# A hybrid decoder layer on eight cores: eleven pre-cast experts instead of ten, gathers requested four steps ahead, and the overflow weights fetched in two parts

## The reference, cut to what matters

```python
h = rmsnorm(x, g_mix); proj = h @ w_in                 # D = 1024, 1792 columns
attn = sliding_window_attention(q, k, v, sinks)         # window 128, 8 heads of 64
lru = rg_lru(causal_conv4(lx)) * gelu(lg)               # 512 channels, associative scan
x = x + concat(rmsnorm(attn), rmsnorm(lru)) @ w_out
h2 = rmsnorm(x, g_ffn)                                  # mixture of experts
g_top  = top1(softmax(h2 @ w_rg)); e_top = top2 of the 8 experts of that group
x = x + sum over the two experts: w_tok * (silu(h2 @ Wg[e]) * (h2 @ Wu[e])) @ Wd[e]
gate = sigmoid(rmsnorm(x, g_ple) @ w_ple_gate)          # per-layer embedding
x = x + gate * (p @ w_ple_proj)
return rmsnorm(x, g_final)
```

## Time and profile before

| what | value |
|---|---|
| median of 3 runs | 1447.66 us (1443.44 to 1447.93) |
| the profiled execution: its own time | 1447.09 us |
| its span on the slowest core (core 4) | 1445.4 us |
| spans of the eight cores | 1414.2 to 1445.4 us |
| PE / DVE / ACT / POOL busy over the span | 76% / 48% / 51% / 33% |
| granted clock of TensorE, mean of core 4 | 0.850 |
| DMA queue of GpSimd (software), of SyncE (hardware) | 57.1% and 20.1% of 16 engines over the span |

### The profile page before, as it was taken

How to read it: one execution, slowest core, us unless ns; L and a number is a source line. 1 busy time by engine, 2 the same in 40 slices (tenths; PEclk the granted TensorE clock), 3 DMA queues, 4 the chain that set the end, 5 groups by cost and what they waited for, 6 DMA issues and landing times.

```text
span 1445.4 us, 24745 instructions; the slowest of 8 cores (1414.2 to 1445.4 us)
## 1 busy us (share of the span) xinstructions
PE 1092.8 (76%) x7740; PEld 722.3 (50%) x7834; DVE 698.8 (48%) x1253; ACT 742.1 (51%) x1392; POOL 483.6 (33%) x576
## 2 busy tenths in 40 slices
PE   2535759988979897267697979988988797681892
PEld 1312225555555555156475757766766575550440
DVE  4879995977777864541121212211212121225853
ACT  4778897887877974012232423333333242224882
POOL 3212132332323333024242434433444243220663
PEclk9766777988978978559799989999999899895896
DMA  8999996963705932408999999999989989888422
GB/s 230 193 190 109 107 109 85 189 115 96 132 9 88 144 106 94 184 21 160 204 195 220 175 216 208 204 187 205 234 190 184 223 156 174 174 276 319 163 117 117
DMA packets 69775, 234.93 MB, mean 163 GB/s; under 512 B 23430, under 2 KB 30342, under 8 KB 51472
## 3 DMA queue, kind: packets, MB, share of 16 engines
q0 software_dynamic: 43984, 134.60, 57.1%
q1 hardware_dynamic: 25664, 98.75, 20.1%
HBM read 415.47 MB, written 101.71 MB: 358 GB/s over the span
## 4 chain that ended last, share of the span: by engine, by line
PE 44%; DMA 20%; issue 11%; DVE 9%; ACT 9%; POOL 4%; SPq 1%; another core or an unknown queue 0%; DVEq 0%; ACTq 0%; POOLq 0%
PE ps L1369 13%; DMA sb_R<-h2scr,sb_R 12%; PE ps L1341 7%; PE ps L967 4%; DMA sb_R<-wall,sb_R 3%; DMA sb_R<-w_pg 3%; PE ps L751 3%; PE ps L1324 2%; PE ps L1004 2%; PE ps L1512 2%; PE ps L841 2%; PE ps L903 1%; DMA sb_R<-xin 1%; PE ps L904 1%; PE ps L1245 1%
## 5 line engine op out<-in xcount | busy, mean ns | idle before, releaser
L1369 PE MATMUL ps<-sb_R 128*128 128x256 bf16 x3008 | 343.0, 275 | 5.3 <-DMA sb_R<-wall,sb_R 3.6
L1369 PEld LDWEIGHTS ps<-sb_R 128*128 128x128 bf16 x3008 | 296.0, 99 | 53.3 <-issue 6.7
L1351 POOL DMA_INDIRECT yscr<-sb_R x94 | 94.6, 1006 | 361.1 <-DVE sb_R L1348 344.9
L1374 DVE TENSOR_TENSOR sb_R<-sb_R,ps 128x512 bf16<-128x512 f32 x94 | 64.7, 688 | 296.9 <-PE ps L1369 268.8
L1327 ACT COPY sb_R<-ps 128x1024 bf16<-128x1024 bf16 x94 | 95.1, 1012 | 191.6 <-PE ps L1324 187.3
L1341 PE MATMUL ps<-sb_R 128*128 128x512 bf16 x706 | 171.2, 396 | 4.9 <-issue 2.1
L1348 DVE COPY sb_R<-ps 128x512 f32<-128x512 f32 x94 | 65.0, 692 | 222.5 <-PE ps L1341 140.2
L1373 ACT ACTIVATE sb_R<-ps 128x512 f32<-128x512 f32 x94 | 56.1, 597 | 224.8 <-PE ps L1369 224.7
L1295 POOL DMA_INDIRECT sb_R<-h2scr,sb_R x94 | 97.7, 1039 | 89.3 <-DVE sb_R L1254 60.9
L1341 PEld LDWEIGHTS ps<-sb_R 128*128 128x128 bf16 x752 | 74.5, 102 | 89.0 <-issue 19.8
L1324 PE MATMUL ps<-sb_id,sb_R 128*128 128x128 bf16 x752 | 58.1, 237 | 63.6 <-DMA sb_R<-h2scr,sb_R 63.1
(11 more groups left out here) (234 smaller groups left out, 2085.6 us busy)
## 6 DMA issues: line engine op xcount, KB each, us to landing
sb_R<-wall POOLq DMA_DIRECT2D x66, 1024.0 KB, 23.1
wbf<-wall POOLq DMA_DIRECT2D x30, 1024.0 KB, 46.0
sb_R<-wbf SPq DMA_DIRECT2D x30, 1024.0 KB, 13.2
sb_R<-xin SPq DMA_DIRECT2D x32, 512.0 KB, 20.3
sb_R<-yscr SPq DMA_DIRECT2D x16, 1024.0 KB, 8.1
xscr<-sb_R SPq DMA_DIRECT2D x16, 512.0 KB, 4.1
sb_R<-xscr SPq DMA_DIRECT2D x16, 512.0 KB, 13.4
out<-sb_R SPq DMA_DIRECT2D x16, 512.0 KB, 2.7
```

Source lines behind the costliest of these rows:

```text
L1351: return e.indirect_dma_start(y_d, bass.IndirectOffsetOnAxis(ap=didx[:, blk:blk + 1], axis=0), y.ap, None, bounds_check=breg(e, 2 * T_OWN ...
L1369: ins = e.matmul(pv[:, q * N:(q + 1) * N], lhsT=w_[:, c, f * P:(f + 1) * P], rhs=hT_[:, c, 0:N], start=(c == 0), stop=(c == 7))
L1374: S.op("dve", lambda e: e.tensor_tensor(hid[s % 2][:, fp * 2:fp * 2 + 2, 0:N], sgs[fp][:, 0:2 * N].rearrange("p (q t) -> p q t", q=2), pu. ...
```

## The change

`PC` becomes eleven experts, without 0 and 1, and spread evenly from 2 to 28; the six that are cast behind tiles go behind tiles 0, 2, 4, 6, 8 and 10. Experts 0 and 1 are read as float32 on GpSimd's queue. Gathered rows get a ring of `NG` = 5 and are requested four steps ahead. `wall` is split into `wgu` (gate and up) and `wdn` (down); `load_ov` has two parts with a dependency each: gate and up are requested behind `gateup(s, 1)` of an overflow step, down behind its `down`. Since a fifth gather buffer moves what lies behind it by 1024 words, `wov` now reaches 384 words into the mixer's `Wout`, and the dispatch's temporaries are moved to the place of `hTs`, `hid`, `sgs` and `Y`, over the mixer's `b1024` and `f512` pools. In the tail only 8 of the 16 `ppT` are made ahead (ring of 8), four behind the first group and four behind the second.

```diff
-        PC = [0, 1, 2, 6, 9, 13, 16, 20, 23, 27]
+        PC = [2, 4, 6, 9, 11, 14, 17, 19, 22, 25, 28]
...
-                    S.dma("pool", wbf_d[E, :, sl], wall_d[E, :, sl], writes=[pc_b[E][i]], sembuf=pcs_b[E], after=[mk], kb=1536)
+                    S.dma("pool", wbf_d[E, :, sl], wgu_d[E, :, sl] if i < 2 else wdn_d[E], writes=[pc_b[E][i]], sembuf=pcs_b[E], after=[mk], kb=1536)
...
-                    if gt - 16 in (0, 3, 5, 8, 10):
+                    if gt - 16 in (0, 2, 4, 6, 8, 10):
                         precast(1, mt)
...
         NWG, NWD = 4, 3
+        NG = 5
+        rtb = B("rtmp"); ut_b = B("utri"); qr_b = B("qr"); OHm1_b = B("OHm")
+        OH_b = [B(f"OH{i}") for i in range(4)]; OHr_b = [B(f"OHr{i}") for i in range(4)]
         wg_b = [B(f"wg{i}") for i in range(NWG)]; wu_b = [B(f"wu{i}") for i in range(NWG)]; wd_b = [B(f"wd{i}") for i in range(NWD)]
-        G_b = [[B(f"G{i}{h}") for h in range(2)] for i in range(4)]
+        G_b = [[B(f"G{i}{h}") for h in range(2)] for i in range(NG)]
         hTs_b = [B("hTs0"), B("hTs1")]; hid_b = [B("hid0"), B("hid1")]; sg_b = [B("sg0"), B("sg1")]
-        wov_b = B("wov")
+        wov_b = B("wov"); wovd_b = B("wovd")
         wgs = [R.alloc(8 * 512, BF16, wg_b[i]).rearrange("p (c f) -> p c f", c=8) for i in range(NWG)]
...
         wds = [R.alloc(4 * D, BF16, wd_b[i]).rearrange("p (c d) -> p c d", c=4) for i in range(NWD)]
+        tmp_off = R.off
         hTs = [R.alloc(8 * 256, BF16, hTs_b[i]).rearrange("p (c t) -> p c t", c=8) for i in range(2)]
         hid = [R.alloc(4 * 256, BF16, hid_b[i]).rearrange("p (c t) -> p c t", c=4) for i in range(2)]
         sgs = [R.alloc(512, F32, sg_b[i]) for i in range(2)]
         YP = R.pool(S, "Y", 1024, 5)
         tail_end = R.off
-        Gb = [R.alloc(2 * D, BF16, *G_b[i]).rearrange("p (h d) -> p h d", h=2) for i in range(4)]
+        Gb = [R.alloc(2 * D, BF16, *G_b[i]).rearrange("p (h d) -> p h d", h=2) for i in range(NG)]
         wov = R.alloc(12288, BF16, wov_b)
+        wovd_b.ranges.append((R.off - 2048, R.off)); wov_b.ranges[0] = (R.off - 6144, R.off - 2048)
...
-        R.off = disp_off
-        rtb = B("rtmp"); ut_b = B("utri")
+        R.off = tmp_off
...
-        rtb.ranges.append((disp_off, R.off)); rtb.older = None
+        assert R.off <= tail_end
+        rtb.ranges.append((tmp_off, R.off))
...
-                    return e.indirect_dma_start(Gb[s % 4][:, h, :], None, h2_d,
+                    return e.indirect_dma_start(Gb[s % NG][:, h, :], None, h2_d,
...
-                S.dmaop("pool", fn, reads=[ix_b] + H2d, writes=[G_b[s % 4][h]], kb=256)
...
-        def load_ov(j):
+                S.dmaop("pool", fn, reads=[ix_b] + H2d, writes=[G_b[s % NG][h]], kb=256)
+        def load_ov(j, part):
             if j >= NOVF:
                 return
+            dst, src, wb = ((wov[:, 0:8192], wgur, wov_b), (wov[:, 8192:12288], wdnr, wovd_b))[part]
             def fn(e):
-                return e.indirect_dma_start(wov, None, wallr,
+                return e.indirect_dma_start(dst, None, src,
                                             bass.IndirectOffsetOnAxis(ap=oidx[:, j:j + 1], axis=0),
                                             bounds_check=breg(e, NE * P - 1), oob_is_err=False)
-            S.dmaop("pool", fn, reads=[ox_b], writes=[wov_b], kb=256)
+            S.dmaop("pool", fn, reads=[ox_b], writes=[wb], kb=256)
         def weights_of(st_):
             if st_[0] == "b":
                 E = st_[1]
                 return wgs[E % NWG], wus[E % NWG], wds[E % NWD], wg_b[E % NWG], wu_b[E % NWG], wd_b[E % NWD]
-            return wov_g, wov_u, wov_d, wov_b, wov_b, wov_b
...
-        S.op("pool", lambda e: e.memset(wov.bitcast(F32), 0.0), writes=[wov_b])
-        for i in range(4):
+        S.op("pool", lambda e: e.memset(wov.bitcast(F32), 0.0), writes=[wov_b, wovd_b])
+        for i in range(NG):
             S.op("pool", lambda e, i=i: e.memset(Gb[i].bitcast(F32), 0.0), writes=G_b[i])
...
-        load_ov(0)
-        load(2)
+        load_ov(0, 0)
+        load_ov(0, 1)
+        for s in range(2, NG - 1):
+            load(s)
         trans(0)
         for s in range(nS):
-            if s + 3 < nS:
-                load(s + 3)
+            if s + NG - 1 < nS:
+                load(s + NG - 1)
...
                 down(s - 1)
                 k, j = steps[s - 1]
                 if k == "o":
-                    load_ov(j + 1)
+                    load_ov(j + 1, 1)
                 elif j + NWD < NE and j + NWD >= NPL:
                     load_wd(j + NWD)
             gateup(s, 1)
             k, j = steps[s]
+            if k == "o":
+                load_ov(j + 1, 0)
             if k == "b" and NPL <= j + NWG < NE:
                 load_w(j + NWG)
...
-        THP = R.pool(S, "thp", 128, 16)
+        THP = R.pool(S, "thp", 128, 8)
         TP = R.pool(S, "tp", 256, 1)
         TH = R.pool(S, "th", 128, 2)
         ppTs = []
-        for ot in range(NT):
+        def pp_tile(ot):
...
+        for ot in range(8):
+            pp_tile(ot)
         for g in range(NT // 4):
             xs, h3s = [], []
...
+            if g < 2:
+                for ot in range(8 + 4 * g, 12 + 4 * g):
+                    pp_tile(ot)
```

More of the change, by code:

```diff
@@ L588, in build @@
     brt_d = dt("b_rt", [1, 36], F32, kind="ExternalInput").ap()
-    wall_d = dt("wall", [NE, P, 12288], F32, kind="ExternalInput").ap()
+    wgu_d = dt("wgu", [NE, P, 8192], F32, kind="ExternalInput").ap()
+    wdn_d = dt("wdn", [NE, P, 4096], F32, kind="ExternalInput").ap()
     cst_d = dt("cst", [P, 2 * P + 41], F32, kind="ExternalInput").ap()
@@ L1134, in build @@
         slots = R.alloc(2 * NT); sli = R.alloc(2 * NT, I32); qi = R.alloc(2 * NT, I32); ri = R.alloc(2 * NT, I32)
-        qf = R.alloc(2 * NT); rf = R.alloc(2 * NT); qr_b = B("qr")
+        qf = R.alloc(2 * NT); rf = R.alloc(2 * NT)
         slots3 = slots.rearrange("p (t k) -> p t k", t=NT)
@@ L1138, in build @@
         OHq = [R.alloc(4 * NB).rearrange("p (j n) -> p j n", j=4) for _ in range(2)]
-        OHm1 = R.alloc(4 * NB).rearrange("p (j n) -> p j n", j=4); OHm = [OHm1, OHm1]; OHm1_b = B("OHm"); OHm_b = [OHm1_b, OHm1_b]
-        OH_b = [B(f"OH{i}") for i in range(4)]; OHr_b = [B(f"OHr{i}") for i in range(4)]
+        OHm1 = R.alloc(4 * NB).rearrange("p (j n) -> p j n", j=4); OHm = [OHm1, OHm1]; OHm_b = [OHm1_b, OHm1_b]
         p1T = R.alloc(NB); inv = R.alloc(NB)
-        rtb.ranges.append((disp_off, R.off)); rtb.older = None
+        assert R.off <= tail_end
+        rtb.ranges.append((tmp_off, R.off))
         for b_ in OH_b + OHr_b + [OHm1_b, qr_b, ut_b]:
-            b_.ranges.append((disp_off, R.off))
+            b_.ranges.append((tmp_off, R.off))
         print("dispatch words", R.off)
@@ L1272, in build @@
                 steps.append(("o", E // 2 - 1))
-        wallr = wall_d.rearrange("e p n -> (e p) n")
+        wgur = wgu_d.rearrange("e p n -> (e p) n")
+        wdnr = wdn_d.rearrange("e p n -> (e p) n")
         Yd = []
@@ L1278, in load_w @@
                 dst = ring[E % NWG]
-                src = (wbf_d if E in PC else wall_d)[E, :, k * 4096:(k + 1) * 4096].rearrange("p (c f) -> p c f", c=8)
+                src = (wbf_d if E in PC else wgu_d)[E, :, k * 4096:(k + 1) * 4096].rearrange("p (c f) -> p c f", c=8)
                 S.dma("sp" if E in PC else "pool", dst, src, reads=pc_b[E] if E in PC else [], writes=[rb[E % NWG]],
@@ L1283, in load_wd @@
         def load_wd(E):
-            src = (wbf_d if E in PC else wall_d)[E, :, 8192:12288].rearrange("p (c d) -> p c d", c=4)
+            src = (wbf_d[E, :, 8192:12288] if E in PC else wdn_d[E]).rearrange("p (c d) -> p c d", c=4)
             S.dma("sp" if E in PC else "pool", wds[E % NWD], src, reads=pc_b[E] if E in PC else [], writes=[wd_b[E % NWD]],
@@ L1313, in weights_of @@
                 return wgs[E % NWG], wus[E % NWG], wds[E % NWD], wg_b[E % NWG], wu_b[E % NWG], wd_b[E % NWD]
-            return wov_g, wov_u, wov_d, wov_b, wov_b, wov_b
+            return wov_g, wov_u, wov_d, wov_b, wov_b, wovd_b
         def trans(s):
@@ L1323, in tr @@
                     for c in range(8):
-                        ins = e.transpose(pt[:, c * P:(c + 1) * P], Gb[s % 4][:, h, c * P:(c + 1) * P], id16[:])
+                        ins = e.transpose(pt[:, c * P:(c + 1) * P], Gb[s % NG][:, h, c * P:(c + 1) * P], id16[:])
                     return ins
-                S.op("pe", tr, reads=[G_b[s % 4][h], id16_b], writes=[pt])
+                S.op("pe", tr, reads=[G_b[s % NG][h], id16_b], writes=[pt])
                 S.op("act", lambda e, h=h, pt=pt: e.copy(hT_[:, :, h * P:(h + 1) * P], pt.ap.rearrange("p (c t) -> p c t", c=8)),
@@ L1542, in make_in_maps @@
     rows = lambda a, nc_, n: f(a)[0].reshape(NE, nc_, P, n).transpose(0, 2, 1, 3).reshape(NE, P, nc_ * n)
-    wall = np.ascontiguousarray(np.concatenate([rows(inp["w_expert_gate"], 8, 512), rows(inp["w_expert_up"], 8, 512),
```

(5 more changed lines are left out.)

## The result

The changed kernel takes 1461.43 us in the median (1452.68 to 1490.88) against 1447.66: the ratio is 1.0092 with an interval of 1.0066 to 1.0118. The highest of its seven executions, 1490.88, is one in which the cores of one die had a lower clock; the other six end at 1464.37. Forecast were 1420 us and a range of 1390 to 1442. It is slower, and the prediction is wrong in sign.

A forecast was written before the change was run, and what follows sets the result against it. The prediction took DMA work in the expert steps as the bound. Its terms, -29 - 6 + 3 + 0 + 0 + 3 + 2 = -27 us, took 1447.1 to 1420 us, range 1390 to 1442.

The forecast's parts named there:

- What bounds the steps: Expert steps: DMA work is the bound, engines 95% busy; waits for gathered rows, 63.1 us, are where it shows.
- More bf16 experts: Expert steps: nine pieces turn from casting to bf16 at 3.2 us each, -29 us (21 to 37 less).
- Gathers four steps ahead: Expert steps: earlier requests help at the tail's loads and the early queue, fewer tail casts too; -6 us (0 to -19).
- Overflow weights in two parts: Expert steps: 15 more indirect DMAs, hidden on POOL, cost DMA time; +3 us (0 to 5).
- The rival of a wait for the overflow's weights: Expert steps: the wait moves to overflow gate and up weights, 24 of 27 us gone, 1444 us; chance 0.16.
- Experts 0 and 1 as casts: Before the steps: their float32 loads are covered by the dispatch with 14 us to spare; 0 us (0 to +10).
- One more pre-cast: Mixer's second half: three more pieces, some 20 us of DMA, fit in 160 us left free; 0 us (0 to +4).
- Moved buffers: Mixer's end and dispatch: later `wov` memset, one more gather memset, dispatch waiting for pools; +3 us (0 to +8).
- Tail: Tail: eight `ppT` tiles made inside it cost ACT 3 us together, loaded one by one; +2 us (0 to 6).
- experts 0 and 1 come too late: Start of the steps: their loads start only at 636, first gather lands at 683; +18 us, 1465 us; chance 0.10.

The follow-up runs named there:

- the list alone: The kernel before with only the list of eleven experts and casts behind tiles 0, 2, 4, 6, 8, 10: 1452.22 us, ratio 1.0028.
- the run with ten casts: The changed kernel with ten listed experts, cast behind the old tiles 0, 3, 5, 8, 10, all else as changed: 1431.56 us, ratio 0.9883.
- the list of ten: The kernel before with only its ten listed experts changed to 2, 4, 6, 9, 11, 14, 17, 20, 23, 27: 1426.59 us, ratio 0.9838.

## Why the prediction was wrong

Step by step, with what each term measured:

- **What bounds the steps: right.** DMA share stayed at 0.95, the steps shrank with the bytes, the waits mostly changed their names (63.1 us for gathered rows became 6.6 and 42.4 for overflow weights), and a third kind of transfer taken away moved most of its wait on to the next. Its bytes are not the whole story: 28 requests that bring nothing were worth 11 us.
- **More bf16 experts, -29 us: right, -26.5** (the list alone; 2.9 us for each of nine pieces, and 3.1 for each of six). The Trainium skill (HBM Reference, Specifications), by whose figure the term was an estimated -26, agrees with that as well.
- **Gathers four steps ahead, -6: wrong sign.** Steps +1.8 in one pair of kernels and -2.2 in the other, which is nothing within what single profiles tell; tail +3.5 and +3.6. The ring of five with its move of `wov` cost 12 us in the full change (1.0006 to 1.0092) and, within the error, 4 in the other pair. Of the 6.2 us of it at the first gather 3.8 are the last router tile, which the prediction had under the moved buffers. The reason given for discounting the term, that full engines only move the wait, was right, and should have taken the rest of it as well: neither the tail's weights nor the early queue gave anything back.
- **Overflow weights in two parts, +3: no cost.** Two pairs of kernels differ in the two parts, their tensors and the moved temporaries alone, and have steps that are 4.3 and 4.6 us shorter with them (613.9 against 618.2, 621.6 against 626.2); one profile each, so a gain is likely and not shown. The rival of a wait for the overflow's weights came true as a wait (42.4 us against the forecast "under 10"), with the gathers four steps ahead (in the two kernels with eleven or ten listed casts and three steps ahead it is at most 14 us on a core): it took the place of the gathers' wait and added nothing that the steps show. What it would save to be without those requests, 11 us, the prediction did not ask.
- **Experts 0 and 1 as casts, 0 (0 to +10): right.** They land during the dispatch, as forecast: the DMA engines are idle from 645 us, 11 us or more ahead of the first gather on every core. The +2.8 us to the first gate and up block come from three cores where PE and ACT are late at a hand-over, by a cause that is open; in the run with ten casts it is +0.4.
- **One more pre-cast, 0 (0 to +4): this is the step that failed, with +29** (28 by the router tiles; 24 go with the bytes of two casts). The term was priced from the mean share of the part (0.53, "leaves 160 us free"). A mean of 0.53 over 341 us says nothing on the 30 us in which a cast and four loads meet. The prediction did say that a cast "could hold up loads of `x`", but of the one behind tile 2, which held up none; the casts that did are the one behind tile 0, which had not moved, and the one behind tile 4, and for the first of them it took a reordering of SyncE's queue that no line of the diff shows. The row to read would have been the landing time of the one load of `x` behind a cast in the kernel before, 25.3 us where the three ahead of the cast took 4.6 to 10.5: four such loads instead of one at the first place, and four instead of none at the second.
- **Moved buffers, +3 (0 to +8): right, +3.7**, as the last router tile's end. Of these 1.8 are the memset; the other 1.9 come with DVE's new order there, which was not foreseen. The dispatch is not longer (55 us from the last router tile to the first gather in both).
- **Tail, +2 (0 to 6): +7.3.** Along the chain of kernels that differ in one step each, the tail is 150.9 us before, 153.6 with the list and the places, 154.2 with the two parts and the moved temporaries, 154.7 with the late `ppT`, and 158.2 with the ring of five. Only the last step, 3.5, is the same in a second pair. The late `ppT` cost 3.6 in another pair, where the list of ten had left the tail at 150.7. Why the ring of five reaches the tail, and how the rest is shared, is open.

The stages add up to +32.5 + 2.8 - 29.2 + 7.3 = +13.4 us for the profiled execution, and the medians differ by 13.8. The rival "experts 0 and 1 come too late" had 1465 us, close to the measured time. That is luck and not what happened: its place was the first gather's landing, 45 us late, and on the four cores whose trace has that landing the gather landed in 3.4 to 3.5 us.

## What to carry to other kernels

A background transfer is not free because its part has idle engines on average. It costs what it delays at the moment when it is in the queue: look at which urgent loads are requested within its drain time (here some 30 us for an expert of three pieces, 244.2 to 275.7 us on core 5), and read the landing times of the ones that already stand behind such a transfer. Put it where the queue is empty and the next urgent load far; here eleven casts cost the mixer some 29 us behind tiles 0, 2, 4, 6, 8 and 10, 21 us with one more in block 1, and nothing with the sixth behind tile 12 and the third behind tile 6.

When an edit moves an instruction in a kernel whose order a scheduler makes, ask which neighbours the scheduler will move in turn, on queues that the diff does not name.

In a stretch where the DMA engines are full, take bytes away first: here each piece of 1 MB read as bf16 instead of float32 gave 2.9 to 3.1 us, while a fourth step of look-ahead gave -2.2 and +1.8 us and only changed the name of what PE waits for. But count requests too: 28 that move nothing were worth 11 us.

## What the runs showed of the hardware

Loads on SyncE's queue and casts on POOL's do not get equal shares of the DMA engines, although they are on queues of their own: 512 KB loads that land in 4.4 to 6.8 us alone took 26.6 to 30.0 us behind three casting pieces of 1 MB and 29.7 to 63.7 behind a longer backlog (core 5). The three casting pieces themselves, requested from 244.2 us, landed in

```profile
DMA to landing us min/median/max: 9.6/18.5/29.8
```

which ends at 275.7 us, and the first of the four loads landed at 275.9. The queues (packets, MB, share) in the changed kernel, first from 250 to 262 us with casts and loads waiting, then from 275 to 282:

```profile
q0 software_dynamic: 182, 1.30, 96.2%
q1 hardware_dynamic: 106, 0.22, 5.2%
```

```profile
q1 hardware_dynamic: 659, 2.20, 94.2%
```

SyncE's queue does move beside the casts, but in packets: 106 in 12 us against 182, and a casting packet takes 1.0 us of an engine where one of SyncE's takes 0.09 (96.2% and 5.2% of 16 engines' 12 us). So it gets a twentieth of the time; when the casts are through it moves 659 packets in 7 us.

The requests for overflow weights bring nothing on this input. The casting and indirect queue over the whole span, core 0 (packets, MB, share), with all of them and with 28 left out:

```profile
q0 software_dynamic: 46144, 134.61, 59.5%
```

```profile
q0 software_dynamic: 42112, 134.60, 60.1%
```

They are 144 packets each and 0.01 MB in all. Still PE waited 32 to 56 us on each core of the changed kernel for five to seven of them, and leaving them out of the kernel with ten casts was worth 11 us of the steps.
